# Up projections of two squared-ReLU stages: one product of 512 columns in place of two of 256

## The reference

```
def squared_relu_mlp(x, w_up, w_down):      # x (256, 1024), w_up (1024, 4096), w_down (4096, 1024)
    h = jax.nn.relu(x @ w_up)
    return (h * h) @ w_down
```

## Time and profile before

| | |
|---|---|
| median of 3 runs | 1230.51 us |
| lowest and highest of them | 1225.38, 1230.92 us |
| time of the profiled execution | 1240.02 us |
| its span (first to last instruction) | 1238.0 us |
| granted TensorE clock, mean | 0.995 |
| PE busy | 97% of the span |
| DVE, ACT busy | 64%, 49% |

### The profile page before, as it was taken

One profiled execution on the slowest core, in us unless ns is written; L12 is line 12 of the kernel. 1 busy time (PEld: TensorE's weight loads), 2 busy tenths in 40 slices (PEclk: granted clock), 3 DMA queues, 4 the chain that ended last, 5 costly groups with the idle time before them and its releaser, 6 DMA issues. The chain is left out here.

```text
span 1238.0 us, 22461 instructions
## 1 busy us (share of the span) xinstructions
PE 1205.2 (97%) x9076; PEld 1019.3 (82%) x9076; DVE 788.2 (64%) x1330; ACT 608.1 (49%) x994; POOL 97.3 (8%) x100
## 2 busy tenths in 40 slices
PE   9999999999999999999999998999999999999997
PEld 7989999999899999898999998899999953333332
DVE  6876655566755556899899989878754573321214
ACT  6665544454644445577765567666545331111112
POOL 0000100000100000000000021001100004233401
PEclk9999999999999999999999999999999999999999
DMA  8654555655355556454544365354553999999995
GB/s 299 204 172 136 177 194 176 201 172 169 111 196 176 193 177 193 137 171 151 174 152 137 92 220 202 110 186 156 171 170 102 362 367 413 417 411 413 413 418 233
DMA packets 160756, 270.00 MB, mean 218 GB/s; under 512 B 17402, under 2 KB 125919, under 8 KB 156574
## 3 DMA queue, kind: packets, MB, share of 16 engines
q1 hardware_dynamic: 149872, 260.53, 59.9%
q0 software_dynamic: 10432, 8.16, 2.2%
q10 hardware_dynamic: 366, 0.12, 0.0%
HBM read 287.89 MB, written 12.58 MB: 243 GB/s over the span
## 5 line engine op out<-in xcount | busy, mean ns | idle before, releaser
L2170 DVE TENSOR_TENSOR weights_parts<-ring,weights_parts 128x1024 fp32r<-128x1024 f32 (+3 forms) x312 | 363.3, 1184 | 147.2 <-ACT weights_parts L1583 146.9
L1583 ACT ACTIVATE weights_parts<-ring 128x1024 fp32r<-128x1024 f32 (+3 forms) x312 | 308.7, 1010 | 154.4 <-PE psum L891 154.1
L889 PE MATMUL psum<-xnorm_parts,weights_parts 128*128 128x256 f32 x852 | 243.5, 286 | 6.0 <-DVE arena L2573 2.2
L890 PE MATMUL psum<-xnorm_parts,weights_parts 128*128 128x256 f32 x852 | 237.8, 279 | 0.0
L891 PE MATMUL psum<-xnorm_parts,weights_parts 128*128 128x256 f32 x852 | 237.8, 279 | 0.0
L889 PE MATMUL psum<-expert_cols,weights_parts 128*128 128x256 f32 (+1 forms) x688 | 195.0, 283 | 3.5 <-DVE expert_cols L2188 2.2
L890 PE MATMUL psum<-expert_cols,weights_parts 128*128 128x256 f32 (+1 forms) x688 | 192.6, 280 | 0.0
L891 PE MATMUL psum<-expert_cols,weights_parts 128*128 128x256 f32 (+1 forms) x688 | 192.6, 280 | 0.0
L889 PE MATMUL psum<-hidden_parts,weights_parts 128*128 128x256 f32 x640 | 181.6, 284 | 3.1 <-DVE hidden_parts L2641 1.7
L890 PE MATMUL psum<-hidden_parts,weights_parts 128*128 128x256 f32 x640 | 179.9, 281 | 0.0
L891 PE MATMUL psum<-hidden_parts,weights_parts 128*128 128x256 f32 x640 | 179.9, 281 | 0.0
(11 more groups left out here) (463 smaller groups left out, 1742.2 us busy)
## 6 DMA issues: line engine op xcount, KB each, us to landing
ring<-in_mlp_w_up SPq DMA_DIRECT2D x32, 1024.0 KB, 5.3
ring<-in_mlp_w_down SPq DMA_DIRECT2D x32, 1024.0 KB, 4.9
ring<-in_w_in SPq DMA_DIRECT2D x30, 1024.0 KB, 5.2
ring<-in_attn_w_qkv SPq DMA_DIRECT2D x12, 1024.0 KB, 5.9
expert_raw<-in_w_exp_gate SPq DMA_DIRECT2D x22, 512.0 KB, 11.0
expert_raw<-in_w_exp_up SPq DMA_DIRECT2D x22, 512.0 KB, 11.8
ring<-in_w_exp_down SPq DMA_DIRECT2D x11, 1024.0 KB, 15.6
expert_raw<-in_w_exp_down SPq DMA_DIRECT2D x9, 1024.0 KB, 15.1
```

The source lines that it names most:

```text
L889: pe.matmul(out, lh, rh, start=start, stop=False, **more)
L890: pe.matmul(out, lh, rl, start=False, stop=False, **more)
L1583: ins = act.activation(high, src, ACT.Copy)
L2170: ins = dve.tensor_tensor(low, src, high.bitcast(F32), ALU.subtract)
```

## The change

The up projections use a new function, `project_wide`. For each slice k it loads the high weights once and multiplies them by both token parts at once, 512 columns: the first 256 columns of the bank get high by high, the last 256 get high by low. A second product, low weights by high tokens, adds to the first 256. Each half of a chunk now has a bank of its own (banks 0 and 1), both are used by every chunk, and the two column halves of a bank are added when it is read: ACT copies the first halves of both banks to `sgate`, DVE adds the second halves (this raises `made[0]`), and a further DVE instruction makes clipped value times value (raises `hid_squared`). Every up n + 1 waits for the add of chunk n, where before it waited for chunk n - 1. The down projections are the same as before.

```diff
-        for b in range(2):
-            self.bank_fills[b] += FC // 2
+        self.bank_fills[0] += FC
...
+        mem_both = moe_cols[:, 0:2 * KT * TOK].rearrange("p (s k t) -> p s k t", s=2, k=KT)
...
+            def project_wide(n, banks, both, xn_from=None, shift=0):
+
+                for m, b in enumerate(banks):
+                    high, low = split_half(n, m, shift)
+                    for k in range(KT):
+                        if xn_from is not None and m == 0:
+                            pe.wait_ge(s["xn_ready"], xn_from + k + 1)
+                        pe.matmul(bank2(b), high[:, k, :], both[:, :, k, :], start=(k == 0), stop=(k == KT - 1),
+                                  skip_group_check=True)
+                        mm = pe.matmul(bank2(b)[:, 0, :], low[:, k, :], both[:, 0, k, :], start=False,
+                                       stop=(k == KT - 1), skip_group_check=True)
+                    mm.then_inc(s["units_done"], 1)
...
                 def up(it, n, xn_from=None):
-                    b = n % 2
-                    pe.wait_ge(made[b], it * 2 + (u[b] + n // 2))
-                    project_split(first + (2 * n - 1 if n else 0), b, xn_from, shift=it * 16, parts=PARTS[2 * i + 1])
+                    pe.wait_ge(made[0], it * 4 + (u[0] + n))
+                    if n == 0:
+                        pe.wait_ge(made[1], u[1])
+                    project_wide(first + (2 * n - 1 if n else 0), (0, 1), mem_both, xn_from, shift=it * 16)
...
-                    act.activation(sgate[:, b, :], bank(b), ACT.Relu).then_inc(s["gate_silu"], 1)
+                    act.activation(sgate[:, b, :].rearrange("p (m t) -> p m t", m=2), psum[:, 0:2, 0:TOK],
+                                   ACT.Copy).then_inc(s["up_copied"], 1)
                     f(2 * n + 1 if n else 2, 1)
-                    act.wait_ge(made[b], it * 2 + (u[b] + n // 2 + 1))
+                    act.wait_ge(s["hid_squared"], it * 4 + (FC * i + n + 1))
...
-                    dve.wait_ge(s["gate_silu"], it * 4 + (FC * i + n + 1))
-                    dve.scalar_tensor_tensor(sgate[:, b, :], bank(b), 0.0, sgate[:, b, :], ALU.max,
-                                             ALU.mult).then_inc(made[b], 1)
+                    dve.wait_ge(s["up_copied"], it * 4 + (FC * i + n + 1))
+                    halves = sgate[:, b, :].rearrange("p (m t) -> p m t", m=2)
+                    dve.tensor_tensor(halves, psum[:, 0:2, TOK:2 * TOK], halves, ALU.add).then_inc(made[0], 1)
+                    dve.wait_ge(made[0], it * 4 + (u[0] + n + 1))
+                    dve.scalar_tensor_tensor(sgate[:, b, :], sgate[:, b, :], 0.0, sgate[:, b, :], ALU.max,
+                                             ALU.mult).then_inc(s["hid_squared"], 1)
```

More of the change, by code:

```diff
@@ L554, in build_two_blocks @@
             "final_ready", "before_ready", "nat_copied",
-            "sq_ready", "xn_ready", "dve_step", "att_max", "exp_done", "p_ready", "rope_done", "gains_set", "gated_folded", "queries_roped", "queries_moved0", "queries_moved1", "hid_ready",
-            "gate_silu", "z_high", "z_low", "srec_ready", "p_second", "dt_ready", "conv_done", "xw_ready", "cs_ready", "ea_ready", "dec_ready",
+            "sq_ready", "xn_ready", "dve_step", "att_max", "exp_done", "p_ready", "rope_done", "gains_set", "gated_folded", "hid_squared", "queries_roped", "queries_moved0", "queries_moved1", "hid_ready",
+            "up_copied", "z_high", "z_low", "srec_ready", "p_second", "dt_ready", "conv_done", "xw_ready", "cs_ready", "ea_ready", "dec_ready",
             "m_ready", "y_ready", "z_tanh", "ssd_roots", "key_in", "kpe_copied", "kpe_roped", "rope_raw", "roped", "tables_moved", "hi_ready",
```

## The result

| | before | changed |
|---|---|---|
| median of the runs (4 each) | 1228.15 us | 1246.26 us |
| lowest to highest | 1225.38 to 1230.92 | 1243.15 to 1247.98 |
| ratio, with its 95% interval | | 1.0132 [1.0095, 1.0168] |
| profiled execution: time, span | 1240.0, 1238.0 us | 1245.04, 1243.0 us |

The changed kernel is 1.3% slower: 18 us, where 3 us less had been forecast. The two profiled executions differ by 5 us only; that these two differences disagree is part of the answer.

What follows compares the result with a forecast made beforehand. PE was taken as the bound within the stages. Slices -9.1, downs -2.6, entry +5.0 and clock +3.4 summed to -3.3 us, so 1227.2 from a median of 1230.5; range 1219 to 1238, the forecast's own 1224 to 1232.

Steps and rivals of the forecast that it cites:

- The entry: Start of each stage: up 1 waits for DVE's add of chunk 0, PE stands 3.5 us; 2.5 us lost per stage, 5.0 together.
- The clock term: During up 1: one fall of the clock to 0.50 per stage after PE's stand, 1.7 us each, 3.4 lost together.
- The cover in the middle of the stages: Mid-stage: 32 new DVE instructions cost nothing, hidden under a whole down projection, with 4 us to spare.
- the passing of a loss to the end: After the stages: what comes later waits for PE, so a gain or loss passes one to one to the end.
- I take 216: Up projections: a 512-column fp32r product lasts 216 ns, read from bf16 and f32 rows, with 251 as the upper end.
- the 9.1 us of gain: Up projections, chunks 2 to 15 of both stages: 448 slices at 331.5 ns each, 21.8 or 8.1 less than before.
- rival (b): Up products: columns set the price, not loads; 512 cost 235.6 ns, a slice 353.4; 1235.5 to 1239 us; chance 0.13.
- the pair is bound by whichever is later: Every load and product pair: a load, 111 ns, is as long as a 256-column product, and the later one sets the time.
- The row that I had ruled out, at 251: The only 512-column fp32r products in the trace, 251 ns, held to be load-bound; as a rival, 1243 us, chance 0.04.
- The estimate worked out from its formula: Up slices by the skill's N / 2.4 + 2.5 ns: 1.1 us gained, 7.3 lost net, near 1238 us.
- Half of each gives 2.6 us gained: Down projections: each chunk draws its rate anew, half slow and half quick; ends 5.8 us gained and 0.6 lost.
- the difference should carry over: Whole kernel: the runs' median is 9.5 us below the profiled 1240.0 us, and stays so after the change.

Runs made afterwards that it cites:

- narrow: Against the changed kernel, the 512-column product split back into two of 256 columns, each with its own weight load; 1232.95 us, ratio 1.0014.
- after_again: The changed kernel run again, unchanged, for its spread and a second trace; 1246.14 us, ratio 1.0163.
- the probe: A kernel of its own with streams of products alone, varying columns, type and load width, writing zeros; 227 ns for 512 fp32r columns, 216 for bf16.
- add_first: Against the changed kernel, DVE does the add of chunk 0 ahead of the half of weights; 1238.24 us, ratio 1.0053.
- wide_free: Against the changed kernel, chunk 0 sums in banks 2 and 3 so up 1 has fresh banks, products turn about; 1239.02 us, ratio 1.006.
- three grouped ones: Changed kernel with eight wide products, then eight narrow: alone 1235.69 us; chunk 0 in banks 2 and 3, 1229.01; also high weights first in other projections, 1230.6.
- experiments 6 and 7: Changed kernel with chunk 0 in banks 2 and 3: products turn about in the first, 1239.02 us; in groups of eight in the second, 1229.01 us.
- before_again: The kernel before run again, unchanged, for its spread and a second profile; 1230.43 us, ratio 0.9972.
- before_grouped: Against the kernel before, each half of an up does its 16 products of high weights first, then the 8 of low; 1231.72 us, ratio 1.0031.
- probe2: A second kernel of streams alone, with more orders and shorter loads, writing zeros; 0.347 us a slice turned about, 0.349 in groups of eight.
- grouped: Against the changed kernel, each half does its 8 wide products first, then the 8 of low weights; 1235.69 us, ratio 1.0042.

## Why the prediction was wrong

**What held.** The entry came out as written: the place, the engine, the instruction behind which DVE is late, and the length (3.44 us for 3.5). That down 0 of stage 0 then came 2.42 us later, for 2.5, is partly luck: up 1 started at 129.48 and not 130.0, and took 5.76 us and not 5.3. With the clock the entries are worth 7.2 us by the medians, for 8.4 summed. The clock term was the least certain: a stand of the same length was followed by no fall, by 3.4 us or by 6.8 us at 0.50 in different entries. Both entries together lost 3.4 us by it in the changed kernel's first profile and in `narrow`, as forecast, and 6.8 in `after_again`. The cover in the middle of the stages held too: 32 more DVE instructions, no wait. So did the passing of a loss to the end: the part behind stage 1 took 731.5 to 732.9 us in the ten profiles other than that of the earlier trace rows.

**The step that failed first: "I take 216".** The price of a 512-column product was read from bf16 and from f32 streams and given to fp32r. Measured: 235 in the kernel, 227 alone. A slice costs 353 and not 331.5, and the 9.1 us of gain are zero. This is rival (b) within a nanosecond: it had 235.6 and 353.4, with a chance of 0.13. That it hit so closely is luck in part, since columns by themselves give 227 and the other 8 ns hang on the order and the loads; and its time, 1239 at the most, is 7 us short for the reason given third. The premise behind the choice, "the pair is bound by whichever is later" with the load as the later one, was wrong: with a load half as long the pair still takes 113. What a full load adds, 7 ns in the probe, lies on top of the columns.
The row that I had ruled out, at 251, was rightly ruled out, but it was the only fp32r row of this width, and it should have warned that the type matters.
By the Trainium skill, TensorE: Matmul & The Clock Gate, section Back-to-back issue gap (N / 2.4 + 2.5 ns, no type named), 512 columns take 216 ns; the bf16 stream of the probe agrees, the fp32r ones, 227 to 235, don't. The section calls this the gap of an isolated product and gives about 131 ns a product for a stream of loads and 512-column products; no stream here came near that, 216 being the least. The estimate worked out from its formula (near 1238, no real gain from the slices) was closer than mine all the same, though its price for the wide product was mine.

**The second: "Half of each gives 2.6 us gained".** I had the downs draw their rate anew in every chunk. They don't: in the eight stages of four profiles with turn-about wide products (the changed kernel twice, `add_first`, `wide_free`) every down from down 1 on ran at 117.8 and every slice at 353; in the six stages of three grouped ones every down from down 1 on ran at 113.3. Down 0 ran at the other rate twice, as told under experiments 6 and 7. With 256-column products alone both rates occur, in the same program. (The count of chunks was off too: downs 12 to 15 of stage 1 were quick before, four and not three. That is 0.2 us.)

**The third: "the difference should carry over".** The profiled execution of before, 1240.0 us, was one at the slow rate nearly throughout; I called it 9.5 us longer than the median and did not ask why. Both rates stood in the earlier trace rows.

Pricing all of it (estimates from the slots in the traces): 2 x 16 x 96 = 3072 products, 4.4 ns apart, are 13.5 us between an execution that is all slow and one that is all quick. In the profile of before some 430 products were quick already (both ups 1, and from up 13 of stage 1 on), which leaves 11.7; and its part behind stage 1 took 734.2 us, 2.3 or so more than elsewhere. Without both, 1240.0 comes down to about 1226, next to the group of runs at 1223.1 to 1226.5. The profiles of `before_again` and `before_grouped` (1230.06 and 1231.17, most of one stage slow, about 5 us) come out at 1225 and 1226 by the same estimate. The changed kernel starts from the slow end always. So the loss is to be counted from the quick end: 1226 + 13.5 (the quick rate, never had) + 7.2 (the entry) = 1247, measured 1246.

The profile of before had the 117.8 ns too, so against it only the entry and the clock count, which is why the two profiles lie just 5 us apart. At the end of stage 1 they were 7.8 us apart (the last product of down 15 starts at 511.54 and before at 503.77): the entries' 8.4 and 1.4 for the lost quick stretch, less 0.4 that the changed kernel's profile was ahead at the first clearing and 1.5 between the stages, where the fall of the clock of the earlier trace rows is missing from the changed kernel's profile. The 2.8 us that came back afterwards are no gain of the change but the long last part of the profile of before, 734.2 us for 731.5.

**What stays open.** What draws the rate for 256-column products, and why turn-about widths hold the slow one. Runs show that in this kernel the order decides for wide products, and that in a stream by itself a shorter load brings the alternation down to 340 ns. That a load under a running stream is what slows it at the slow rate is an argument from the probes; the second of them did not reproduce the gain of grouping, and nothing here shows the mechanism.

## What to carry to other kernels

Before merging two products into a wide one, look for a row of the same type and width, and if there is none, price it by the column at the rate that the kernel has: here the 512 loads that went gave nothing back. If the trace shows two rates for the same instructions, find out at which one the timed runs are before carrying a difference from a profile to a median: a change can win nothing at the one rate and still lose the other. And where one bank pair takes the place of two that alternate, look at the first round, where the work that covered the read isn't there yet; spare banks for that one round were worth 7 us here.

## What the runs showed of the hardware

- fp32r streams have a price per column of 0.443 ns (113 ns for 256, 227 for 512) with loads of 64 columns in the probes, higher than that of bf16 (216 for 512, 0.422). In the kernel the 256-column products come at 113.3 or at 117.8 ns (0.46 a column), each for tens to hundreds of us at a granted clock of 1.00.
- The order of the same 16 products moved a stage from one price to the other: turn about 235 + 118 ns, in groups of eight 234 + 114, and with it the 256-column downs behind them, 117.8 against 113.3. In a stream by itself (`probe2`) the same grouping made no difference, 349 ns a slice for 347.
- Between down 0 and down 15 of eight stages of 256-column products the rate changed three times, each time at up 13, behind the L869 rows that break into the stream, and never in the loop before.
- A pair with 128 columns takes 111 ns, one with 256 columns 120 in the probe with a full load and 113 with a load of 64 columns.
- The granted clock after a stand of 3.4 us of PE was 1.00 (stage 0 of the changed kernel's first profile), 0.50 for 3.4 us (`narrow`, both entries) or 0.50 for 6.8 us (stage 1 of that profile; `after_again`, both entries). After stands of 2.7 us it was 1.00 once and 0.50 for 3.4 us once (`grouped`); after stands of 1.4 to 1.5 us (`add_first`) it was not seen to fall.
